# A 96-token tile searched first and the third tile's gates built one group per weight tile, in a transformer layer with a sparse expert FFN

## The reference, cut to what matters

```python
x = x + gate1 * mix(rms_norm(x) * (1 + scale1) + shift1)       # attention part, untouched
h2 = rms_norm(x, norm2_g) * (1.0 + scale2) + shift2            # [512 tokens, 1024]
q = (h2 @ w_query).reshape(T, 8, 2, 64)
s = einsum('thpd,hpnd->thpn', q, sub_keys)                     # 128 keys a side
s_top, i_top = top_k(s, 16)                                    # "search", first half
cand = s_top[:, :, 0, :, None] + s_top[:, :, 1, None, :]
best, bi = top_k(cand.reshape(T, 8, 256), 16)                  # "search", second half
e = i_top0[bi // 16] * 128 + i_top1[bi % 16]                   # 128 experts a token of 16384
g = softmax(best)
a = gelu(einsum('tkd,td->tk', u_table[e], h2))
x = x + gate2 * einsum('tk,tkd->td', g * a, v_table[e])        # y
```

## Time and profile before

| | |
|---|---|
| median of 3 runs | 1413.74 us (1413.10 to 1415.67) |
| profiled execution, span of its instructions | 1406.0 us |
| time outside that span, if the profiled run took the median | 7.7 us |
| TensorE, VectorE, GpSimd, ScalarE busy | 97%, 85%, 55%, 50% |
| granted TensorE clock, mean of the span | 0.996 (full in every slice after the first) |
| DMA | 438.8 MB, mean 312 GB/s; about 400 GB/s in the v stage |

### The profile page before, as it was taken

One profiled execution on the slowest core, in us unless ns is written; L12 is line 12 of the kernel. 1 busy time (PEld: TensorE's weight loads), 2 busy tenths in 40 slices (PEclk: granted clock), 3 DMA queues, 4 the chain that ended last, 5 costly groups with the idle time before them and its releaser, 6 DMA issues.

```text
span 1406.0 us, 23810 instructions
## 1 busy us (share of the span) xinstructions
PE 1369.2 (97%) x8569; PEld 1267.3 (90%) x8569; DVE 1198.2 (85%) x2667; ACT 709.0 (50%) x1325; POOL 775.0 (55%) x465
## 2 busy tenths in 40 slices
PE   6999889999999999999999999999999999999999
PEld 2465556889999999999999999899999999999999
DVE  5767878677999889899998866599999989999997
ACT  1245874334436884488637853443434334443442
POOL 0000000104698877788787878676756668567660
PEclk9999999999999999999999999999999999999999
DMA  9830101565699999999999999999999999999996
GB/s 353 318 118 0 61 1 61 177 242 196 212 315 347 332 339 371 413 363 323 352 408 357 340 346 408 395 363 402 395 393 402 386 372 402 399 399 397 402 400 224
DMA packets 158230, 438.83 MB, mean 312 GB/s; under 512 B 16608, under 2 KB 50720, under 8 KB 156832
## 3 DMA queue, kind: packets, MB, share of 16 engines
q1 hardware_dynamic: 91632, 244.55, 47.5%
q0 software_dynamic: 46080, 167.79, 30.9%
q10 hardware_dynamic: 20400, 24.95, 5.0%
HBM read 390.02 MB, written 47.22 MB: 311 GB/s over the span
## 4 chain that ended last, share of the span: by engine, by line
PE 72%; DVE 12%; DMA 7%; issue 4%; ACT 2%; POOL 1%; SPq 1%; DVEq 0%; ACTq 0%
PE ps L1329 11%; PE ps L1331 11%; PE ps L1330 11%; PE ps L1380 6%; PE ps L1381 6%; PE ps L1382 6%; PE ps L1340 6%; PE ps L1023 5%; DVE y_tok L1894 4%; DMA raw<-in_v_tiles 3%; DVE lo L1881 2%; DMA act_in<-gelus 2%; DMA qkc<-in_w_ada 1%; DVE cf L1870 1%; PE ps L1181 1%
## 5 line engine op out<-in xcount | busy, mean ns | idle before, releaser
L866 ACT ACTIVATE hi<-raw 128x1024 fp32r<-128x1024 f32 x256 | 270.7, 1058 | 211.3 <-DMA raw<-in_v_tiles 139.8
L583 POOL TENSOR_TENSOR lo<-raw,hi 128x1024 fp32r<-128x1024 f32 x123 | 297.2, 2418 | 143.0 <-ACT hi L866 142.3
L1329 PE MATMUL ps<-h2hi,hi 128*128 128x352 f32 x1024 | 335.3, 327 | 2.9 <-POOL lo L583 2.9
L1331 PE MATMUL ps<-h2hi,lo 128*128 128x352 f32 x1024 | 330.5, 323 | 0.0
L1330 PE MATMUL ps<-h2lo,hi 128*128 128x352 f32 x1024 | 330.4, 323 | 0.0
L1380 PE MATMUL ps<-chi,hi 128*128 128x352 f32 x1008 | 324.3, 322 | 0.1
L1381 PE MATMUL ps<-clo,hi 128*128 128x352 f32 x1008 | 324.2, 322 | 0.0
L1382 PE MATMUL ps<-chi,lo 128*128 128x352 f32 x1008 | 324.2, 322 | 0.0
L596 POOL DMA_INDIRECT row_res<-in_v_tiles,E x91 | 175.3, 1927 | 103.9 <-DVE y_tok L1894 70.5
L1329 PEld LDWEIGHTS ps<-h2hi,hi 128*128 128x128 f32 x1024 | 193.0, 189 | 4.9 <-POOL lo L583 4.6
L1330 PEld LDWEIGHTS ps<-h2lo,hi 128*128 128x128 f32 x1024 | 192.7, 188 | 0.0
(11 more groups left out here) (311 smaller groups left out, 2161.9 us busy)
## 6 DMA issues: line engine op xcount, KB each, us to landing
raw<-in_u_tiles SPq DMA_DIRECT2D x128, 512.0 KB, 6.0
raw<-in_v_tiles SPq DMA_DIRECT2D x128, 512.0 KB, 7.8
gelus<-act_out ACTq DMA_DIRECT2D x128, 176.0 KB, 5.8
act_in<-gelus SPq DMA_DIRECT2D x128, 176.0 KB, 9.3
gates<-stage SPq DMA_DIRECT2D x32, 512.0 KB, 8.1
gate<-gates SPq DMA_DIRECT2D x32, 512.0 KB, 9.2
late<-in_w_ada SPq DMA_DIRECT2D x4, 2048.0 KB, 7.9
qkT<-in_w_ada SPq DMA_DIRECT2D x3, 2048.0 KB, 20.5
```

Source lines behind the costliest of these rows:

```text
L583: nc.gpsimd.tensor_tensor(lo[m % 3][:], raw[m % 3][:], hi[m % 3][:].bitcast(F32), ALU.subtract).then_inc(u_lo, 1)
L866: nc.scalar.activation(hi[m % 3][:], raw[m % 3][:], ACT.Copy).then_inc(t_hi, 1)
L1329: nc.tensor.matmul(out, hi[n % 3][:, cols], dense(h2hi, k), start=(k == 0), stop=False)
L1331: last = nc.tensor.matmul(out, lo[n % 3][:, cols], dense(h2hi, k), start=False, stop=(k == KD - 1))
```

## The change

`TORD` becomes (3, 2, 0, 1): the tile with 96 dense and 32 extra tokens is searched and built at p = 1. Its gates get a buffer and a DRAM tensor of 96 columns (`stage_few`, `gates[1]`). The builds of p = 1 and 2 keep two groups a weight tile (12 and 16 tiles, n = 28 to 39 and 57 to 72); the third takes one group a tile over 32 tiles, n = 90 to 121; `tail_at` = 122. The extra tokens' numbers are ready at n = 28, so all 160 row dots follow one another, the last at n = 121, with the turn of the extra tokens before tile 105. `FILL` goes from 9, 10, 10 to 10, 12, 12. `own_low` is every third tile from 93 to 120. In `search`, several small tiles move to PSUM. The third tile's gates, now full, stay in `stage`, and ScalarE copies them into the `gate` buffer, four v tiles at a time (`copy_resident`), so that `weigh` is one product over 384 columns, 32 of them zero. `y_tok` moves to other memory, and six memsets are added before the v stage.

```diff
-TORD = (3, 0, 1, 2)
+TORD = (3, 2, 0, 1)
...
+        (stage_few,), _ = region(at0, [("stage_few", [P, NT, P - XT], F32)])
         (stage,), at_c = region(at0, [("stage", [P, NT, P], F32)])
+        stages = {p: stage_few if TORD[p] == ND - 1 else stage for p in range(1, TT)}
...
+        groups_of = {p: (P - XT if TORD[p] == ND - 1 else P) // HB for p in range(1, TT)}
+        GROUPS_A_TILE = {p: 2 if p < TT - 1 else 1 for p in range(1, TT)}
...
-        FILL, PAUSES, LAST = {1: 9, 2: 10, 3: 10}, 15, NT - 4
+        FILL, PAUSES, LAST = {1: 10, 2: 12, 3: 12}, 15, NT - 4
+        turn_at = build_at[TT - 1] + 15
...
+            if p < TT - 1:
+                rows_at[n] = 3 if (n - build_at[p]) % 4 == 3 else 2
+            elif n == turn_at - 1:
+                rows_at[n] = SLOTS - done
+            else:
+                rows_at[n] = 0 if n == turn_at else min(2, SU - done)
...
-        own_low = [tail_at + 4 + 3 * j for j in range(5)]
+        own_low = list(range(build_at[TT - 1] + 3, tail_at, 3))
...
                 if n % GB == 0:
                     b = n // GB
-                    sp.dma_start(gate[b % 2][:], gates[:, :, n:n + GB, :].rearrange("a p i t -> p a i t")).then_inc(gate_in[b % 2], 16)
+                    for p in range(1, TT - 1):
+                        sp.dma_start(gate[b % 2][:, TORD[p], :, 0:stages[p].shape[2]], gates[p][:, n:n + GB, :]).then_inc(gate_in[b % 2], 16)
...
+            def copy_resident(b):
+                if b >= 2:
+                    act.wait_ge(c_mul, GB * (b - 1))
+                nc.scalar.activation(gate[b % 2][:, TORD[TT - 1], :, :], stage[:, b * GB:(b + 1) * GB, :], ACT.Copy).then_inc(resident, 1)
...
+                    if n == turn_at:
+                        turn_tokens(y_tok, 2)
                     dot(n)
-                    for half in range(2):
-                        token_gates(p, i, half)
+                    for c in cs:
+                        token_gates(p, c)
...
-                nc.vector.tensor_copy(sixf[:], six[:])
+                nc.vector.tensor_copy(sixf, six[:])
+                settled(nc.vector.tensor_copy(first_ps, sv[:, 0, :, :]))
...
-                settled(nc.vector.tensor_copy(qr[:], bia[:]))
+                nc.vector.tensor_copy(qr[:], bia[:])
+                settled(nc.vector.tensor_copy(qr_ps, bia[:, 1, :, :]))
...
+                    if n == build_at[1]:
+                        settled(expert_numbers())
+                        nc.vector.tensor_copy(Ef[:].bitcast(U32), Ef[:]).then_inc(more_ready, 1)
+                    if n + 1 in own_low:
+                        low_u(n + 1)
+                    if n == turn_at - 3:
+                        tt_(y_tok[:].rearrange("p (k t r) -> p k t r", k=KD, r=XR), gathered_more(h2hi).bitcast(F32),
+                            gathered_more(h2lo).bitcast(F32), ALU.add).then_inc(x_cols, 1)
+                    fill(rows_at[n])
...
-                tt_(c[:, 0:sent].rearrange("p (a t) -> p a t", t=P), a[:, 0:sent].rearrange("p (a t) -> p a t", t=P),
-                    gate[b % 2][:, :, r, :], ALU.mult)
-                tt_(c[:, sent:TD], a[:, sent:TD], stage[:, n, 0:TD - sent], ALU.mult).then_inc(c_mul, 1)
+                tt_(cf[n % 2][:].rearrange("p (a t) -> p a t", t=P), act_in[n % 4][:].rearrange("p (a t) -> p a t", t=P),
+                    gate[b % 2][:, :, r, :], ALU.mult).then_inc(c_mul, 1)
```

More of the change, by code:

```diff
@@ L435, in build, with group @@
         v_rows = v_tiles.rearrange("n p d -> (n p) d")
-        def group(p, i, half):
-            return (p - 1) * 2 * BUILD + 2 * i + half
-        NGROUPS = 2 * sum(steps_of.values())
+        def group(p, c):
+            return first_group[p] + c
+        NGROUPS = first_group[TT]
+        assert all(g % 2 == 0 for g in first_group.values())
         def dense(of, k):
@@ L1332, in dot, with token_gates @@
                 last.then_inc(a_ps, 1)
-            def token_gates(p, i, half):
-                q = group(p, i, half)
+            def token_gates(p, c):
+                q = group(p, c)
+                half = q % 2
                 pe.wait_ge(oh_ready, q + 1)
@@ L1831, in _, with low_u @@
             g = 0
+            def low_u(m):
+                dve.wait_ge(t_hi, m + 1)
+                tt_(lo[m % 3][:], raw[m % 3][:], hi[m % 3][:].bitcast(F32), ALU.subtract).then_inc(own_lo, 1)
             def fill(count):
                 nonlocal g
-                for _ in range(min(count, SLOTS - g)):
+                for _ in range(count):
                     row_dot(g)
@@ L1895, in row_sum @@
                                                    op0=ALU.mult, op1=ALU.add).then_inc(row_used, 1)
-            dve.wait_ge(oh_used, NGROUPS + 2)
-            tt_(y_tok[:].rearrange("p (k t r) -> p k t r", k=KD, r=XR), gathered_more(h2hi).bitcast(F32), gathered_more(h2lo).bitcast(F32), ALU.add)\
-                .then_inc(x_cols, 1)
-            for g in range(SLOTS, SU):
-                m = tail_at + 3 + (g - SLOTS) // 2
-                if (g - SLOTS) % 2 == 0 and m in own_low:
-                    dve.wait_ge(t_hi, m + 1)
-                    tt_(lo[m % 3][:], raw[m % 3][:], hi[m % 3][:].bitcast(F32), ALU.subtract).then_inc(own_lo, 1)
-                row_dot(g)
+            for b in range(4):
+                nc.vector.memset(act_in[b][:, TD:ND * P], 0.0)
+            for b in range(2):
+                last = nc.vector.memset(gate[b][:, ND - 1, :, P - XT:P], 0.0)
+            settled(last)
             dve.wait_ge(aa_gelu, 1)
```

169 lines of the change are left out of this document (95 added, 74 removed).

## The result

The change makes the kernel slower: 1421.97 us median of 5 runs (1417.02 to 1424.70) against 1413.64 us of 5 runs of before (1412.79 to 1415.67), ratio 1.0077 [1.0057, 1.0097], some 8 us where 4.7 us less were forecast. The same kernel run again beside other ones gave 1.0057 [1.0036, 1.0079]. The profiled execution took 1421.5 us with a span of 1419.6 us, so 1.9 us lie outside the span, not 7.7: the trace shown of before was of an execution about 5 us faster than its neighbours. The two traces therefore also differ where nothing was changed.

What follows compares the result with a forecast made beforehand. TensorE, busy for 97% of the span, was taken to bound the kernel. The only nonzero term, -4.7 us in the tail, took the median from 1413.7 to 1409.0 us, with a range of 1407.6 to 1413.0 us.

Steps and rivals of the forecast that it cites:

- The tail: Last u tiles: TensorE's wait for GpSimd's `lo` goes because GpSimd keeps up; term -4.7 us.
- Work of TensorE: Gate groups only change place, matmuls stay the same; cost 0, at most 1.3 us if each change-over has a fixed price.
- VectorE and ScalarE in the third build: Both engines less loaded than in a two-group step; step 104 tightest, with 3.3 us spare; cost 0.
- Weighing: In the v stage, `weigh` as one product of 384 columns lies near 550 ns, hidden beside busy TensorE.
- The v stage: Smaller gate pieces cost the DMA queues about the same, 22.5 against 22.3 us over 16 engines; term 0.
- the 23 us of spare: V-stage DMA could rise from 389 GB/s to the tail's 408, 5% of 478 us.
- Rival B: Small pieces choke the v stage; at 62 ns a piece TensorE loses 18 us, 1427 us total; chance 0.12.
- point of decision: V-stage piece price from which choking decides, about 44 ns; from 49 ns the kernel gets slower.
- DMA of the u stage: Beside the third search, 12 row gathers instead of 10 delay transfers about 1.3 us, absorbed; cost 0, bound 1.3.
- the lead of `lo`: Beside the third search, the 3 us by which `lo` runs ahead absorbs the DMA delay of about 1.3 us.
- The search at p = 1: Added row dot and copies are paid by PSUM operands; cost 0, late by 1.3 us if nothing is saved.
- Rivals A: Part of the wait returns in searches, gate changes or DMA; two or more losses give 1411.6 to 1412.9 us, chance 0.13.

Runs made afterwards that it cites:

- v_512: Changed kernel with the 96-column gates loaded into a separate buffer as 512-byte pieces and weighed in two products; ratio 1.0079, v stage 484.3 us.
- b_384: Kernel before, its v-stage gates load split in two and the second cut to 96 of 128 columns, landing in 384-byte pieces; ratio 1.0024.
- all_four: Changed kernel with one-hots weighed before `hi`, first v loads spread, expert numbers at second search, gates packed in 1536-byte pieces; 1405.81 us against 1409.74.

## Why the prediction was wrong

*The tail* (-4.7 us): right, in mechanism and size. *Work of TensorE*: right, a tile with one group takes 4.73 us, no fixed price. *VectorE and ScalarE in the third build*: right for VectorE (tile 104 with the turn behind it loses the same 0.9 us that tile 106 lost before). For ScalarE only its load was counted, not its order. *Weighing*: 552 ns for the single product, where some 550 were forecast.

*The v stage* (term 0): the step that failed most, 7 us. The price of a 384-byte piece was right (22 ns taken, 23.4 measured). Two things beside it were wrong. The 2 KB pieces issued with the small ones slowed from 88.5 to 110.8 ns, 4096 x 22.3 / 16 = 5.7 us that the sum didn't have; with the 1.3 us by which the small pieces' 24.0 us exceed the 22.7 of those they replaced, that is 7.0, and the stage lost 6.9. That the two agree so well is partly luck: the row gathers took 4.3 us more too (4 KB from 165.2 to 168.7 ns), some 3 to 6 us of the whole cost nothing, and the same code lost between 4.1 and 8.2 us over six traces. And the 23 us of spare, read from 408 GB/s in the tail against 389, did not exist: by the table above it was some 3 to 6 us. The rate of another mix of transfers is no reserve of this one. Rival B was thus the right mechanism with a point of decision that was too high: with their neighbours' loss laid on them the small pieces cost 23.4 + 5.7 us x 16 / 16384 = 29 ns, far under its 44 to 49, and its 18 us were 7. The Trainium skill's page "DMA: Bandwidth & Descriptors" (Specifications) wants at least 512 B a transfer for line rate. These runs show such a border only in the 2 KB pieces beside the small ones (110.8 ns beside 384 bytes, 93.6 beside 512); the stage of v_512, at the border, lost just as much (484.3 against 484.8 us): here the number of pieces on a nearly full queue decided.

*DMA of the u stage* (0, bound 1.3): 1.4 to 3.9 us at tile 90. The debt was foreseen, and the lead of `lo` did take it. What was missed is a second reader of the same late tile: `hi` stands in ScalarE's queue ahead of the one-hots that TensorE wants now. The lead was worked out for the data and not for what is queued behind the wait.

*Not in the sum at all*: the first v loads, moved by `tail_at` from plain tiles into the end of a build (1.2 to 5.8 us), and `expert_numbers`, moved out of the wait behind a search to between two steps of a build (1.1 to 1.7 us at tile 29). Both are moves that the diff shows in one line.

*The search at p = 1* (0, bound 1.3): 0.3 to 1.0 us. The cast did get short, 2.46 to 0.43 us, but another small instruction of the same search now met a subtraction of GpSimd's and grew from 0.69 to 2.41 us (L1825; L1783 before). It started at 423.83 us, 0.14 us after the subtraction, and ended 0.15 us after it:

```profile
423.69 2.40 POOL L610 TENSOR_TENSOR lo<-raw,hi 128x1024 fp32r<-128x1024 f32 x1 [0.34 <-ACT hi L893]
```

So 2.0 us were saved and 1.7 given back; with the row dot (1.2) and the two copies (0.6) added and 0.5 us of spare, that makes the 1.0 us.

The u stage came out even or somewhat longer (578.4 to 583.0 us in the six traces with its code unedited, 578.2 to 580.0 in three with before's and 584.2 in b_384), the v stage gave 7 us, and the last store landed 3.2 us after its issue instead of 2.0. Rivals A and B both happened; they were treated as apart. The forecast gain of 4.7 us and the 4.5 us of all_four are alike partly by chance: in all_four the tail's gain stands against 1.0 us at tile 27.

## What to carry over

Where a DMA share is 1.0, a better rate elsewhere is no measure of the spare: price every added piece, and what it does to the transfers issued beside it, in full. When a wait gets shorter or moves, list what stands behind it in the same engine's program, since the data's own consumer may be the last to suffer. A constant that places several steps (`tail_at`) moves all of them; go through each queue that reads it.
